# Output projection of the mixing stage: fp32 matmuls replaced by three fp16 products of high and low halves

## The chip, the cores and the metric

The kernel runs on one core of one Trainium2 chip, as one program. The metric is the device time of one execution in microseconds (us). Engine names: PE is TensorE's matmuls, PEld its weight loads, DVE is VectorE, ACT is ScalarE, POOL is GpSimd, SP is SyncE, which here only issues DMAs.

## The reference, cut to what matters

The kernel computes one layer of a hybrid encoder for 4096 prompt frames and 128 frames of eight running streams: a mixing layer, then a mixture of experts, then a norm. What is computed around the change:

```
mixed = concatenate([out_a, o], axis=-1)      # (tokens, 1024): 512 from the LRU group, 512 from the delta-rule heads
x = x + mixed @ w_out                         # w_out: 1024 x 1024, float32
x = x + hier_moe(rmsnorm(x, ln2_g), ...)      # the router reads the normed x
```

`o` is the output of a recurrence over tokens (`gdn_sequence`): each block of tokens needs a triangular inverse and the state that the block before left.

## The kernel before

`build` runs phases one after the other: `project_phase` (input projection, groups of 512 tokens), `mix_phase` (this change), routing, experts, `combine_phase`.

`project_phase` already computes its own projection as three fp16 products: PE lines L292 multiply high by high, low by high and high by low halves of 128x512 tiles. ACT makes the high halves of the weights, DVE the low halves (L467), from a staged fp32 copy.

`mix_phase` handles 33 tiles of 128 tokens (the last one holds the streams). A tile passes three steps, in three consecutive turns: X prepares it (Gram matrices, and a triangular inverse by doubling: levels 1, 2, 4 to 64), Y applies the state and projects, R norms, routes and writes the tile's rows. In one turn the kernel interleaves X of tile t+2, Y of tile t+1 and R of tile t. The order is written out by hand in the list `MIX`: each entry `step.name.engine` is issued in that order on its engine, for each turn. Tiles 0 and 1 and the last ones are written out; those between run in a loop whose body holds two turns (`program`). Each step waits on counters of the steps that it needs (`at(name, t, back)`), so an engine that is ahead waits.

Names that the prediction uses:

- The doubling. `W2`, `W4` to `W64` (PE, L844): product of a masked matrix `Bs` and `Tm`. `I2` to `I64` (DVE, L1166): copies the result out into `WI`, adding the identity. `T2` to `T32` (PE, L854): product of `Zm` and `WI`. `T2c` and so on (ACT, L995, for T1c L991): copies it out into `Tm`. `Z2` to `Z32` (PE, L860): transposes of `Tm`. `Z2c` and so on (ACT, L1003): copies them out into `Zm`. So one level is W, I, T, Tc, Z, Zc, then the next T.
- `outA0` to `outA3` (PE, L923): projection of the LRU half of the features, `ft[p]`, two of the four 128-row chunks and one half of 512 columns each. `outB0` to `outB7` (PE, L935): the heads' half, one head and one column half each, from `mx`. Both accumulate into the banks `YD`, `YE`. In PE's order these stand between the steps of the doubling: one outB between Z and T, one between T and W.
- `oT` (PE, L930) transposes the normed head outputs, `mx` (DVE, L1228) multiplies them by the gate. `o` (DVE, L1221), `so` (ACT, L1025, sums of squares), `ro` (POOL), `on` (DVE, L1225) are the norm before that.
- `x2` (DVE, L1235, L1236) adds the residual, `st` (ACT) stores it and sums squares, `r2` (POOL) and `xn` (DVE, L1241) norm it, `hT0`, `hT1` (PE) and `hc0`, `hc1` (DVE, L1245) turn it for the router `lg` (PE, L947). `h2` (POOL, L1087) is the product that is stored for the experts.
- `S` (DVE, L1214) updates the state, `G` (DVE, L1147) builds the decayed Gram matrix, `Z1` (DVE, L1161 and L1163) starts the doubling, `B2` to `B64` (POOL, L1065) mask `G` for each level. `ATm` (POOL, L1059) masks the attention matrix. `T1` (PE, L833) and `T1c` start the doubling of the tile; `r0`, `r1` (DVE) pick the experts.
- SP issues, in this order: `ft[0]`, router, norm row, token numbers, `xr[0]`, `w_out` (4 MB), the streams' states `S_s` (2 MB, needed by the last tile alone), then in its loop `ft` and `xr` of tile 1 and those that follow (L752 to L758). `ft` of tile t+2 waits until `outA1` and `mx` of tile t are done.

Of the kernel before, what the change touches and what calls it, by code (L numbers as in the profile page):

```python
# [16 lines left out]
FP16 = mybir.dt.float16  # L17
# [559 lines left out]
Y.N.pe Y.vd.dve Y.vh.act  # L577
X.kt.pe X.ktc.act X.vt.pe X.sc.dve
R.hT0.pe R.hT1.pe R.hc0.dve R.hc1.dve
Y.dS.pe Y.S.dve Y.AV.pe  # L580
# [5 lines left out]
X.W2.pe X.I2.dve Y.outA0.pe  # L586
X.T2.pe X.T2c.act Y.outA1.pe Y.oT.pe X.B8.pool
X.W4.pe X.Z2.pe X.Z2c.act Y.mx.dve X.I4.dve Y.outB0.pe X.B16.pool
X.T4.pe X.T4c.act Y.outB1.pe X.B32.pool
X.W8.pe X.Z4.pe X.Z4c.act X.I8.dve R.r3.dve Y.outB2.pe  # L590
# [12 lines left out]
def mix_phase(nc, T, gb, const, cols, eid, rank, wts, base):  # L603
    NT = tiles()
    H = HEADS
    with ExitStack() as ctx:
        def sb(name, shape, dt=FP32):
            return ctx.enter_context(nc.sbuf_tensor(name, shape, dt))

        def sem(name):  # L610
            return ctx.enter_context(nc.semaphore(name))

        w_out = sb("w_out", [P, KD, D])
        router = sb("router", [P, KD, P])
# [73 lines left out]
        flat = lambda b: b[:, :, :].rearrange("p h n -> p (h n)")  # L688

        done = {(st, e): Steps(sem(f"mix_{st}_{e}"), [n for a, n, b in MIX if a == st and b == e], lead=2)  # L690
                for st in "XYR" for e in ENGINES if any(a == st and b == e for a, n, b in MIX)}
        owner = {n: done[st, e] for st, n, e in MIX}
        weights_in = sem("mix_weights_in")
        w_out_in = sem("w_out_in")
        S_s_in = sem("S_s_in")
# [14 lines left out]
        def at(name, t, back=0):  # L710
            return owner[name].at(name, t, back)
# [12 lines left out]

        def program(engine, begin, x_step, y_step):
# [24 lines left out]
        @block.sync  # L750
        def _(sp):
            def load(t, p):  # L752

                sp.wait_ge(*at("outA1", t, 2))
                sp.wait_ge(*at("mx", t, 2))
                sp.dma_start(ft[p][:, :, :], T["mixin"][:, :, bass.ts(t, P)]).then_inc(ft_in[p], 16)
                sp.wait_ge(*at("x2", t, 2))
                sp.dma_start(xr[p][:, :], T["x"][bass.ts(t, P), :]).then_inc(xr_in[p], 16)  # L758

            sp.dma_start(ft[0][:, :, :], T["mixin"][:, :, 0:P]).then_inc(ft_in[0], 16)  # L760
            sp.dma_start(router[:, :, :], T["router"]).then_inc(weights_in, 16)
            sp.dma_start(ln2_row[:, :], T["ln2_row"].to_broadcast([P, D])).then_inc(weights_in, 16)
            sp.dma_start(tok[:, :], T["tokens"]).then_inc(weights_in, 16)
            sp.dma_start(xr[0][:, :], T["x"][0:P, :]).then_inc(xr_in[0], 16)
            sp.dma_start(w_out[:, :, :], T["w_out"]).then_inc(w_out_in, 16)
            sp.dma_start(S_s[:, :, :, :], T["S_s"]).then_inc(S_s_in, 16)
            with sp.Fori(0, (NT - 1) // 2) as pair:
                load(pair * 2 + 1, 1)
                load(pair * 2 + 2, 0)
            sp.wait_ge(S_ready, 1)  # L770
            sp.dma_start(T["out_S_p"], S[:, :, :]).then_inc(S_out, 16)
            sp.wait_ge(S_ready, 2)
            sp.dma_start(T["out_S_s"], S_s[:, :, :, :]).then_inc(S_out, 16)
            sp.wait_ge(S_out, 32)
# [6 lines left out]
        def _(pe):  # L781
# [87 lines left out]
            def y_step(n, t, p, stream, did):  # L869
# [46 lines left out]
                elif n[:-1] == "outA":  # L916
                    half, c0 = divmod(int(n[-1]), 2)
                    if isinstance(t, int) and t == 0:
                        pe.wait_ge(w_out_in, 16)
                    pe.wait_ge(*at("x2", t, 1))  # L920
                    pe.wait_ge(*at("r0" if half == 0 else "hc1", t, 1))
                    for c in (2 * c0, 2 * c0 + 1):
                        ins = nc.tensor.matmul(flat((YD, YE)[half]), ft[p][:, QC + ZC + c, :],  # L923
                                               w_out[:, c, half * 512:half * 512 + 512], start=(c == 0), stop=False)
                    ins.then_inc(*did(n))
# [35 lines left out]
        def _(act):  # L961
# [43 lines left out]
            def y_step(n, t, p, stream, did):  # L1005
# [12 lines left out]
                elif n == "so":  # L1018
# [88 lines left out]
        def _(dve):  # L1107
# [68 lines left out]
            def y_step(n, t, p, stream, did):  # L1176
# [734 lines left out]
```

## Time and profile before

| | |
|---|---|
| Time, median of 3 runs (lowest to highest) | 4360.78 us (4359.83 to 4360.94) |
| The profiled execution, its span | 4364.01 us, 4362.4 us |
| PE, PEld busy (share of the span) | 3795.3 us (87%), 2252.1 us (52%) |
| DVE, ACT, POOL busy | 1899.5 us (44%), 1409.7 us (32%), 843.1 us (19%) |
| Mixing stage | from about 1250 to 2960 us |

A row of the groups by line reads: line, engine, operation, output<-inputs, shapes, xcount | busy us, mean ns of one | idle us of the engine just before them <- what ended it. A row of the timeline reads: start us, duration us, engine, line, operation, names, shapes, xcount [idle before <- releaser]. Rows with a count are merged. An fp32 matmul leaves two records. Matmuls are pipelined: their recorded durations overlap the next one, so a price per matmul is read from start to start.

### The profile page before, as it was taken

The numbers are of one execution on the slowest core, as the hardware profiler recorded it, in microseconds if no ns is written. First come the engines' busy times: TensorE is split into PE (matmuls) and PEld (weight loads), VectorE is DVE, ScalarE is ACT, GpSimd is POOL, SyncE is SP. The second block draws the span as 40 slices with busy tenths as digits, with TensorE's granted clock in tenths as the row PEclk, the third lists the DMA queues.
The fourth block names the chain that finished last, engine by engine and source line by source line (L and its number), as shares of the span: only waits on it lengthen the run. The fifth ranks groups of instructions, "written<-read, shape, count | busy, mean of one in ns | idle before, by whom it ended". The sixth has DMA issues, their size and how long they took to land. (4 is left out here: it accounts for less than half of the span.)

```text
span 4362.4 us, 64251 instructions
## 1 busy us (share of the span) xinstructions
PE 3795.3 (87%) x19068; PEld 2252.1 (52%) x19069; DVE 1899.5 (44%) x4556; ACT 1409.7 (32%) x2749; POOL 843.1 (19%) x853
## 2 busy tenths in 40 slices
PE   7999999999959899889989998965999999999920
PEld 3444444444556666666666676652444444444410
DVE  6555545644535555555555555533111111111147
ACT  6445444544433333333333333300111111111122
POOL 0000000000013333343333333311111111111145
PEclk9999999999979999999999999977999999999965
DMA  4210111010131121112112111103554545553269
GB/s 148 88 66 33 55 48 67 36 53 34 47 121 49 58 65 60 57 59 64 63 56 66 56 63 58 54 20 136 190 186 173 202 178 197 192 186 131 96 276 383
DMA packets 221781, 454.94 MB, mean 104 GB/s; under 512 B 20818, under 2 KB 132818, under 8 KB 213074
## 3 DMA queue, kind: packets, MB, share of 16 engines
q1 hardware_dynamic: 138498, 220.96, 14.9%
q10 hardware_dynamic: 54288, 146.56, 8.5%
q0 software_dynamic: 28864, 86.09, 5.6%
q14 instruction: 100, 0.82, 0.1%
q8 instruction: 31, 0.51, 0.0%
HBM read 303.84 MB, written 149.71 MB: 104 GB/s over the span
## 5 line engine op out<-in xcount | busy, mean ns | idle before, releaser
L1539 PE MATMUL ebank<-w,rowsT 128*128 x1568 | 711.6, 608 | 35.6 <-SPq L1489 32.3
L292 PE MATMUL pP<-h_hi,w_hi 128*128 128x512 f16 (+1 forms) x1728 | 625.0, 366 | 31.5 <-DVE h_lo L474 16.8
L292 PE MATMUL pP<-h_hi,w_lo 128*128 128x512 f16 (+1 forms) x1728 | 624.6, 365 | 0.0
L292 PE MATMUL pP<-h_lo,w_hi 128*128 128x512 f16 (+1 forms) x1728 | 624.5, 365 | 0.0
L1539 PEld LDWEIGHTS ebank<-w,rowsT 128*128 128x128 f32 x1568 | 303.9, 195 | 429.1 <-issue 429.1
L1557 PE MATMUL ebank<-w,guT 128*128 x784 | 353.4, 593 | 2.6 <-ACT guT L1578 2.6
L1606 DVE TENSOR_TENSOR gu<-ebank,sil 128x256 f32<-128x256 f32 x98 | 41.6, 425 | 707.2 <-ACT sil L1574 707.2
L505 DVE SCALAR_TENSOR_TENSOR cv<-win,cols_sb,cv 128x512 f32<-128x512 f32 (+1 forms) x432 | 305.4, 707 | 35.1 <-issue 3.6
L1574 ACT ACTIVATE sil<-ebank 128x256 f32<-128x256 f32 x98 | 37.7, 385 | 829.7 <-PE ebank L1539 829.6
L1166 DVE TENSOR_TENSOR WI<-bank,const 128x512 f32<-128x512 f32 x198 | 136.5, 690 | 376.4 <-PE bank L844 371.9
L292 PEld LDWEIGHTS pP<-h_hi,w_hi 128*128 128x128 f16 x1728 | 172.0, 100 | 220.7 <-issue 30.8
L1065 POOL TENSOR_TENSOR B<-G,const 128x512 f32<-128x512 f32 x198 | 255.8, 1311 | 143.8 <-DVE G L1147 138.8
L844 PEld LDWEIGHTS bank<-Tm,B 128*128 128x128 f32 x1584 | 195.0, 194 | 158.8 <-ACT Tm L995 78.5
L935 PE MATMUL bank<-w_out,mx 128*128 128x512 f32 x528 | 269.5, 594 | 0.8 <-DVE mx L1228 0.8
L292 PEld LDWEIGHTS pP<-h_lo,w_hi 128*128 128x128 f16 x1728 | 172.2, 100 | 187.6 <-issue 13.6
L844 PE MATMUL bank<-Tm,B 128*128 128x128 f32 x1584 | 228.0, 288 | 46.7 <-ACT Tm L991 42.8
L292 PEld LDWEIGHTS pP<-h_hi,w_lo 128*128 128x128 f16 x1728 | 172.1, 100 | 183.0 <-issue 3.0
L923 PE MATMUL bank<-w_out,ft 128*128 128x512 f32 x528 | 247.9, 593 | 0.0
L854 PEld LDWEIGHTS bank<-WI,Zm 128*128 128x128 f32 x1320 | 162.1, 193 | 141.9 <-ACT Zm L1003 71.8
L854 PE MATMUL bank<-WI,Zm 128*128 128x128 f32 x1320 | 192.5, 289 | 47.1 <-DVE WI L1166 33.2
L252 POOL TENSOR_TENSOR ss<-ss,eps 128x4 f32<-128x4 f32 (+1 forms) x9 | 1.8, 200 | 1115.4 <-ACT junk L340 1115.4
L1557 PEld LDWEIGHTS ebank<-w,guT 128*128 128x128 f32 x784 | 140.9, 189 | 143.7 <-issue 143.7
(282 smaller groups left out, 5703.2 us busy)
## 6 DMA issues: line engine op xcount, KB each, us to landing
w<-in_w SPq DMA_DIRECT2D x32, 2048.0 KB, 9.1
y<-yb ACTq DMA_DIRECT2D x98, 512.0 KB, 4.8
ft<-mixin SPq DMA_DIRECT2D x33, 1280.0 KB, 6.3
mixin<-qo ACTq DMA_DIRECT2D x128, 256.0 KB, 2.0
w<-in_w SPq DMA_DIRECT2D x32, 1024.0 KB, 12.3
xt<-in_x SPq DMA_DIRECT2D x33, 512.0 KB, 6.0
xr<-in_x SPq DMA_DIRECT2D x33, 512.0 KB, 4.7
x<-x2b ACTq DMA_DIRECT2D x33, 512.0 KB, 5.0
```

The source lines that it names most:

```text
L292: ins = nc.tensor.matmul(pP[n % NPB][:, 0:N], w[:, k, c0:c0 + P], h[:, k, 0:N], start=(k + i == 0), stop=(k == KD - 1 and i == 2))
L505: ins = nc.vector.scalar_tensor_tensor(dst, window(c, j, stream), cw(j), dst, ALU.mult, ALU.add)
L844: ins = nc.tensor.matmul(XB[:, h, :], Bs[s][:, h, :], Tm[:, h, :], start=True, stop=True)
L854: ins = nc.tensor.matmul(XC[:, h, :], Zm[:, h, :], WI[:, h, :], start=True, stop=True)
L923: ins = nc.tensor.matmul(flat((YD, YE)[half]), ft[p][:, QC + ZC + c, :], w_out[:, c, half * 512:half * 512 + 512], start=(c == 0), stop=False)
L935: nc.tensor.matmul(flat((YD, YE)[half]), mx[:, h, :], w_out[:, LC + h, half * 512:half * 512 + 512], start=False, stop=(h == H - 1)).then_ ...
L1065: nc.gpsimd.tensor_tensor(Bs[s][:, :, :], G[:, :, :], heads(mat(f"level{s}")), ALU.mult).then_inc(*did(n))
L1166: nc.vector.tensor_tensor(WI[:, :, :], XB[:, :, :], heads(mat("ident")), ALU.add).then_inc(*did(n))
L1539: ins = nc.tensor.matmul((M0, M1)[p][:, :], xT[p][:, k, :], w13[:, bass.ds(s, 1), k * 512:(k + 1) * 512].rearrange("p a n -> p (a n)"), st ...
L1557: ins = nc.tensor.matmul((OA, OB)[h][:, :], guT[p][:, k, :], w.rearrange("p a n -> p (a n)"), start=(k == 0), stop=(k == FE // P - 1))
L1574: nc.scalar.activation(sil[p][:, :], (M0, M1)[p][:, 0:FE], ACT.Silu).then_inc(*did(n))
L1606: nc.vector.tensor_tensor(gu[p][:, :], (M0, M1)[p][:, FE:2 * FE], sil[p][:, :], ALU.mult).then_inc(*did(n))
```

## The change

`w_out` is kept as two fp16 arrays of the same total size, `w_out_hi` (512 times the matrix, rounded) and `w_out_lo` (the rest). Its fp32 form is loaded in two halves into the space of `kz` and `S_s`, which the last tile uses; it is split after the first turn (X of tile 0): eight ACT copies and eight DVE subtractions of 128x1024, each engine in its own order. SP waits for the end of the split before it loads `S_s`, and its `ft` loads come behind that.

For each tile, ACT rounds the LRU features (times 4) to `f_hi` (`fh`) and DVE subtracts for `f_lo` (`fl`); ACT rounds `mx` (`mh`) and DVE subtracts (`ml`). Each fp32 matmul of outA and outB becomes three fp16 matmuls. `x2` becomes a multiplication and an addition. `ft` no longer waits for `outA1`. In PE's order `outA1` moves behind `Z2`, and `outB0` behind `T4`, next to `outB1`.

```diff
-X.kt.pe X.ktc.act X.vt.pe X.sc.dve
-R.hT0.pe R.hT1.pe R.hc0.dve R.hc1.dve
+X.kt.pe X.ktc.act X.vt.pe X.sc.dve Y.fh.act
+R.hT0.pe R.hT1.pe R.hc0.dve R.hc1.dve Y.fl.dve
@@
-X.T2.pe X.T2c.act Y.outA1.pe Y.oT.pe X.B8.pool
-X.W4.pe X.Z2.pe X.Z2c.act Y.mx.dve X.I4.dve Y.outB0.pe X.B16.pool
-X.T4.pe X.T4c.act Y.outB1.pe X.B32.pool
+X.T2.pe X.T2c.act Y.oT.pe X.B8.pool
+X.W4.pe X.Z2.pe X.Z2c.act Y.mx.dve Y.mh.act X.I4.dve Y.outA1.pe Y.ml.dve X.B16.pool
+X.T4.pe X.T4c.act Y.outB0.pe Y.outB1.pe X.B32.pool
@@ program
             run((0, 0, False), None, None)
+            if after_first:
+                after_first()
@@ SP
-                sp.wait_ge(*at("outA1", t, 2))
                 sp.wait_ge(*at("mx", t, 2))
@@
-            sp.dma_start(w_out[:, :, :], T["w_out"]).then_inc(w_out_in, 16)
+            for n, half in enumerate(w_out_raw):
+                sp.dma_start(half, T["w_out"][:, n * 4:n * 4 + 4, :]).then_inc(w_out_in[n], 16)
+            sp.wait_ge(w_out_ready, KD)
             sp.dma_start(S_s[:, :, :, :], T["S_s"]).then_inc(S_s_in, 16)
@@ PE
-                        pe.wait_ge(w_out_in, 16)
-                    pe.wait_ge(*at("x2", t, 1))
+                        pe.wait_ge(w_out_ready, KD)
+                    pe.wait_ge(*at("fl", t))
                     pe.wait_ge(*at("r0" if half == 0 else "hc1", t, 1))
                     for c in (2 * c0, 2 * c0 + 1):
-                        ins = nc.tensor.matmul(flat((YD, YE)[half]), ft[p][:, QC + ZC + c, :],
-                                               w_out[:, c, half * 512:half * 512 + 512], start=(c == 0), stop=False)
+                        for i, (w, f) in enumerate(((w_out_hi, f_hi), (w_out_lo, f_hi), (w_out_hi, f_lo))):
+                            ins = nc.tensor.matmul(flat((YD, YE)[half]), f[:, c, :],
+                                                   w[:, c, half * 512:half * 512 + 512], start=(c + i == 0), stop=False)
@@
-                    pe.wait_ge(*at("mx", t))
+                    pe.wait_ge(*at("ml", t))
@@ ACT
+                elif n == "fh":
+                    act.wait_ge(ft_in[p], ft_turn(t, p))
+                    act.wait_ge(*at("outA1", t, 1))
+                    nc.scalar.activation(f_hi[:, :, :], ft[p][:, QC + ZC:FC, :], ACT.Copy, scale=M_SCALE).then_inc(*did(n))
+                elif n == "mh":
+                    act.wait_ge(*at("outB7", t, 1))
+                    act.wait_ge(*at("mx", t))
+                    nc.scalar.activation(mx_hi[:, :, :], mx[:, :, :], ACT.Copy).then_inc(*did(n))
@@
+            def split_out():
+                for k in range(KD):
+                    act.wait_ge(w_out_in[k // 4], 16)
+                    nc.scalar.activation(w_out_hi[:, k, :], w_out_raw[k // 4][:, k % 4, :], ACT.Copy, scale=W_SCALE
+                                         ).then_inc(w_out_hi_ready, 1)
@@ DVE
+                elif n == "ml":
+                    dve.wait_ge(*at("mh", t))
+                    nc.vector.tensor_tensor(mx_lo[:, :, :], mx[:, :, :], mx_hi[:, :, :], ALU.subtract).then_inc(*did(n))
+                elif n == "fl":
+                    dve.wait_ge(*at("fh", t))
+                    nc.vector.scalar_tensor_tensor(f_lo[:, :, :], ft[p][:, QC + ZC:FC, :], M_SCALE, f_hi[:, :, :],
+                                                   ALU.mult, ALU.subtract).then_inc(*did(n))
@@
-                    nc.vector.tensor_tensor(x2b[:, 0:512], flat(YD), xr[p][:, 0:512], ALU.add)
-                    nc.vector.tensor_tensor(x2b[:, 512:], flat(YE), xr[p][:, 512:], ALU.add).then_inc(*did(n))
+                    nc.vector.scalar_tensor_tensor(x2b[:, 0:512], flat(YD), OUT, xr[p][:, 0:512], ALU.mult, ALU.add)
+                    nc.vector.scalar_tensor_tensor(x2b[:, 512:], flat(YE), OUT, xr[p][:, 512:], ALU.mult, ALU.add
+                                                   ).then_inc(*did(n))
@@
+            def split_out():
+                for k in range(KD):
+                    dve.wait_ge(w_out_hi_ready, k + 1)
+                    nc.vector.scalar_tensor_tensor(w_out_lo[:, k, :], w_out_raw[k // 4][:, k % 4, :], W_SCALE,
+                                                   w_out_hi[:, k, :], ALU.mult, ALU.subtract).then_inc(w_out_ready, 1)
```

## Rows read from the trace of the kernel before

**Rows 1.** The page's costliest groups: the heads' half of the projection.

```profile
L935 PE MATMUL bank<-w_out,mx 128*128 128x512 f32 x528 | 269.5, 594 | 0.8 <-DVE mx L1228 0.8
```

**Rows 2.** Timeline of PE, tile 0's doubling, no projection between the steps.

```profile
1301.41 0.60 PE L860 MATMUL bank<-const,Tm 128*128 128x128 f32 x4
1302.79 1.13 PE L854 MATMUL bank<-WI,Zm 128*128 128x128 f32 x8 [0.78 <-ACT Zm L1003]
1304.70 1.13 PE L844 MATMUL bank<-Tm,B 128*128 128x128 f32 x8 [0.78 <-ACT Tm L995]
```

**Rows 3.** Timeline of PE, tile 1's doubling, an outB between the steps.

```profile
1337.80 0.60 PE L860 MATMUL bank<-const,Tm 128*128 128x128 f32 x4
...
1339.18 1.13 PE L854 MATMUL bank<-WI,Zm 128*128 128x128 f32 x8
1340.14 1.02 PE L935 MATMUL bank<-w_out,mx 128*128 128x512 f32 x2
1341.09 1.13 PE L844 MATMUL bank<-Tm,B 128*128 128x128 f32 x8
```

**Rows 4.** Timeline of PE, a turn in the loop: T2, oT, W4, Z2, T4, W8.

```profile
2003.63 1.16 PE L854 MATMUL bank<-WI,Zm 128*128 128x128 f32 x8 [0.51 <-DVE WI L1166]
...
2006.35 0.60 PE L930 MATMUL bank<-const,onb 128*128 128x128 f32 x4
2006.79 1.06 PE L844 MATMUL bank<-Tm,B 128*128 128x128 f32 x8
2007.68 0.60 PE L860 MATMUL bank<-const,Tm 128*128 128x128 f32 x4
...
2008.98 1.15 PE L854 MATMUL bank<-WI,Zm 128*128 128x128 f32 x8
...
2010.82 1.15 PE L844 MATMUL bank<-Tm,B 128*128 128x128 f32 x8
```

**Rows 5.** Timeline of ACT, the same turn: T4c.

```profile
2010.16 0.60 ACT L995 ACTIVATE Tm<-bank 128x512 f32<-128x512 f32 x1 [1.25 <-PE bank L854]
```

**Rows 6.** Timeline of PE, the same turn: T1 and W2 with their waits.

```profile
1996.55 0.66 PE L833 MATMUL bank<-const,Zm 128*128 128x128 f32 x4 [0.96 <-DVE Zm L1163]
...
2000.24 1.16 PE L844 MATMUL bank<-Tm,B 128*128 128x128 f32 x8 [1.31 <-ACT Tm L991]
```

**Rows 7.** Timeline of DVE: x2's second half, Z1's first part, mx, and on one turn later.

```profile
1982.20 0.68 DVE L1236 TENSOR_TENSOR x2b<-bank,xr 128x512 f32<-128x512 f32 x1
...
1994.00 1.73 DVE L1161 TENSOR_TENSOR B<-G,const 128x512 f32<-128x512 f32 x1 [0.16 <-issue]
...
2006.99 0.75 DVE L1228 SCALAR_TENSOR_TENSOR mx<-bank,cols_sb,ft 128x512 f32<-128x512 f32 x1 [3.41 <-PE bank L930]
...
2050.82 1.76 DVE L1225 TENSOR_TENSOR onb<-ob,ro 128x512 f32<-128x512 f32 x1
```

**Rows 8.** Timeline of POOL, the same turn: B2, then B8 to B64.

```profile
1993.92 1.27 POOL L1065 TENSOR_TENSOR B<-G,const 128x512 f32<-128x512 f32 x1 [4.17 <-DVE G L1147]
...
2004.06 4.95 POOL L1065 TENSOR_TENSOR B<-G,const 128x512 f32<-128x512 f32 x4
```

**Rows 9.** Timeline of PE, input projection: two fp16 matmuls in a run.

```profile
600.25 0.38 PE L292 MATMUL pP<-h_lo,w_hi 128*128 128x512 f16 x1
600.47 0.38 PE L292 MATMUL pP<-h_hi,w_lo 128*128 128x512 f16 x1
```

**Rows 10.** Groups by line and form: DVE's low half of 128x1024 weights.

```profile
L467 DVE SCALAR_TENSOR_TENSOR w_lo<-stage,w_hi 128x1024 f16<-128x1024 f32 x24 | 29.2, 1221 | 11.0 <-ACT w_hi L348 11.0
```

**Rows 11.** Timeline of ACT: sq of tile 1, directly behind Z64c of tile 0.

```profile
1308.76 1.05 ACT L966 ACTIVATE sqb<-ft 128x1024 f32<-128x1024 f32 x1
```

**Rows 12.** The page's DMA issues: KB each, median us from issue to landing.

```profile
ft<-mixin SPq DMA_DIRECT2D x33, 1280.0 KB, 6.3
```

**Rows 13.** Windows: PE, PEld, DVE, ACT, POOL busy, granted clock, DMA share, GB/s.

```profile
1256.00:1280.00 24.00, 13.19 (x70) 12.09 (x71) 6.77 (x22) 5.24 (x10) 9.87 (x7) 0.64 1.03 407
```

**Rows 14.** Timeline of PE, first work of the mixing stage.

```profile
1261.78 3.75 PE L793 MATMUL bank<-const,sqb 128*128 128x128 f32 x16 [17.54 <-DVE gs L1115]
```

More of the change, by code:

```diff
@@ L44 @@
 PROJ = 1.0 / (W_SCALE * H_SCALE)
+M_SCALE = 4.0
+OUT = 1.0 / (W_SCALE * M_SCALE)
 W13, W2 = KD * 2 * FE, (FE // P) * D
@@ L611, in sem @@
             return ctx.enter_context(nc.semaphore(name))
-        w_out = sb("w_out", [P, KD, D])
+        w_out_hi = sb("w_out_hi", [P, KD, D], FP16)
+        w_out_lo = sb("w_out_lo", [P, KD, D], FP16)
+        f_hi = sb("f_hi", [P, LC, P], FP16)
+        f_lo = sb("f_lo", [P, LC, P], FP16)
+        mx_hi = sb("mx_hi", [P, H, P], FP16)
+        mx_lo = sb("mx_lo", [P, H, P], FP16)
+        ng4 = sb("ng4", [P, 1])
         router = sb("router", [P, KD, P])
@@ L688, in mix_phase @@
         flat = lambda b: b[:, :, :].rearrange("p h n -> p (h n)")
+        w_out_raw = [kz[:, :, :, :].rearrange("p h s n -> p (h s n)").rearrange("p (k n) -> p k n", k=4),
+                     S_s[:, :, :, :].rearrange("p s h n -> p (s h n)").rearrange("p (k n) -> p k n", k=4)]
         done = {(st, e): Steps(sem(f"mix_{st}_{e}"), [n for a, n, b in MIX if a == st and b == e], lead=2)
@@ L693, in mix_phase @@
         weights_in = sem("mix_weights_in")
-        w_out_in = sem("w_out_in")
+        w_out_in = [sem(f"w_out_in{n}") for n in range(2)]
+        w_out_hi_ready = sem("w_out_hi_ready")
+        w_out_ready = sem("w_out_ready")
         S_s_in = sem("S_s_in")
@@ L723, in col, with program @@
             return cols[:, COLS[name][0] + n:COLS[name][0] + n + w]
-        def program(engine, begin, x_step, y_step):
+        def program(engine, begin, x_step, y_step, after_first=None):
             for (st, e), d in done.items():
@@ L932, in y_step @@
                 elif n[:-1] == "outB":
-                    pe.wait_ge(*at("mx", t))
+                    pe.wait_ge(*at("ml", t))
                     half, h = divmod(int(n[-1]), H)
-                    nc.tensor.matmul(flat((YD, YE)[half]), mx[:, h, :], w_out[:, LC + h, half * 512:half * 512 + 512],
-                                     start=False, stop=(h == H - 1)).then_inc(*did(n))
+                    for i, (w, f) in enumerate(((w_out_hi, mx_hi), (w_out_lo, mx_hi), (w_out_hi, mx_lo))):
+                        ins = nc.tensor.matmul(flat((YD, YE)[half]), f[:, h, :],
+                                               w[:, LC + h, half * 512:half * 512 + 512],
+                                               start=False, stop=(h == H - 1 and i == 2))
+                    ins.then_inc(*did(n))
                 elif n in ("hT0", "hT1"):
@@ L1042, in y_step @@
                     nc.scalar.activation(exd[:, NGR:], dif[:, NGR:], ACT.Exp).then_inc(*did(n))
-            program("act", act, x_step, y_step)
+            def split_out():
[3 more added lines that the diff above has]
+                                         ).then_inc(w_out_hi_ready, 1)
+            program("act", act, x_step, y_step, split_out)
         @block.gpsimd
@@ L1227, in y_step @@
                     dve.wait_ge(*at("oT", t))
-                    nc.vector.scalar_tensor_tensor(mx[:, :, :], YC[:, :, :], col("ng"), ft[p][:, QC:QC + ZC, :],
+                    dve.wait_ge(*at("mh", t, 1))
+                    nc.vector.scalar_tensor_tensor(mx[:, :, :], YC[:, :, :], ng4[:, 0:1], ft[p][:, QC:QC + ZC, :],
                                                    ALU.mult, ALU.mult).then_inc(*did(n))
+                elif n == "ml":
[5 more added lines that the diff above has]
+                                                   ALU.mult, ALU.subtract).then_inc(*did(n))
                 elif n == "x2":
@@ L1320, in _ @@
             dve.sem_inc(x2_out, 16)
+            nc.vector.tensor_scalar(ng4[:, :], col("ng"), M_SCALE, None, ALU.mult)
             dve.drain()
-            program("dve", dve, x_step, y_step)
+            def split_out():
[3 more added lines that the diff above has]
+                                                   w_out_hi[:, k, :], ALU.mult, ALU.subtract).then_inc(w_out_ready, 1)
+            program("dve", dve, x_step, y_step, split_out)
             dve.drain()
```

## The prediction

> **What bounds the kernel now.** The page comes first. PE is busy 87% of the span, and the projection's second half is one of its larger groups, with only 0.8 us of idle time before it in the whole run [rows 1]. Read alone, this says that PE is full and that every matmul saved is time saved. The timeline says otherwise. Tile 0 goes through the doubling with no projection in between: from Z to T it takes 1302.79 - 1301.41 = 1.38 us, from T to W 1304.70 - 1302.79 = 1.91 us, and PE waits 0.78 us in each for ACT's copy [rows 2]. Tile 1 goes through the same steps with an outB in each place: 1339.18 - 1337.80 = 1.38 us and 1341.09 - 1339.18 = 1.91 us [rows 3]. An outB costs nothing there; it lies in the wait for the copy. In the loop the steps are 2008.98 - 2007.68 = 1.30 us and 2010.82 - 2008.98 = 1.84 us [rows 4], and T4c, which W8 needs, runs from 2010.16 to 2010.76 [rows 5], so W8 starts 0.06 us behind it. PE has a filler that just fits, no queue.
>
> Third, the waits before T1, W2 and T2: 0.96 us for DVE's `Zm`, 1.31 us for ACT's `Tm`, 0.51 us for DVE's `WI` [rows 4, 6]. outA2, outA3 and outA0 are the work directly ahead of these three. So what sets the turn is a chain through DVE and ACT (x2, st, r2, xn, the scales, hc, S, G, Z1, o, so, T1c, then the levels of the doubling), and PE is only a link of it.
>
> **The matmuls that become shorter.** From T2 to oT lie eight records of T2 and four of outA1: 2.72 us [rows 4]. The eight of W4 take 2007.68 - 2006.79 = 0.89 us; those of a T about 0.98. That leaves 1.74 us for four records, 0.43 each, two to a product: 0.87 us. A fp16 matmul of this width follows the one before it in 600.47 - 600.25 = 0.22 us [rows 9], three take 0.65. PE is given back 0.22 us a product, 16 products and 3.5 us a tile, about 115 us in 33 tiles. Of that, outA2, outA3 and outA0 only lengthen waits that are there already, and the outB of the levels from 8 up lie in the waits for Tc and Zc: gain 0. The bounds are 0.02 us a step for these (what separates filler and copy), so at most 0.2 us a tile, and the full 3.5 if I read the chain wrongly (a rival below).
>
> **The part that is rearranged, T2 to W8.** Now 2010.82 - 2003.63 = 7.19 us [rows 4]. After: W4 no longer stands behind outA1, only behind oT (0.44 us), so its own chain sets it, 1.84 us behind T2 instead of 3.16. Z2 follows 0.89 later, its transposes take 0.44, outA1 1.30: T4 at T2 + 4.47 (its chain would allow 1.84 + 0.89 + 1.30 = 4.03). T4 takes 0.98, outB0 and outB1 1.30: W8 at T2 + 6.75 (its chain: 6.31). That is a gain of 0.44 us, if outB0 doesn't wait. It now waits for `ml`: Z2c ends at T2 + 3.97, `mh` takes 0.60 like the other copies of 512 columns, `ml` 0.68 like x2's [rows 7], so T2 + 5.3, just ahead of 5.45. `mh` has T4c behind it in ACT's order, which can't start before T2 + 5.65; `ml` has I8 behind it, which is later. `mx` gets a wait for `mh` of the tile before, long past.
>
> But POOL is at B8 to B64 until 2009.01, which is T2 + 5.38 [rows 8]. Z1's product reads two arrays in SBUF like `ml`; it began 0.08 us behind B2 and took 1.73 us, until 0.54 us after B2 was done, though `mx`, with one input in SBUF, took its 0.75 us in the middle of POOL's work [rows 7, 8]. So `ml` ends near T2 + 5.92, outB0 starts at 5.97, W8 at 7.27: a loss of 0.08. In the other turn of the loop's two, `on` is held up this way already (1.76 us instead of 0.68), T2 comes 1.1 us later, and POOL is done before `ml`: there the gain of 0.44 stands. Mean: -0.18 us a tile.
>
> The Trainium skill, page "SBUF — State Buffer", section "Who interferes with whom", has this as a rule: a DVE instruction with two SBUF inputs and a GpSimd instruction that reads SBUF exclude each other, and the one that issues first holds the ports for its whole length. The trace agrees, with the 1.73 us of Z1's product. Without the rule the two turns would both gain 0.44 and the sum below would be 8 us lower.
>
> **Additions to the chain.** `fl` stands in DVE's order between hc1 and S, and S, G, Z1, o, r0, r1, on and I2 are queued behind it; DVE goes through them with no wait that it could use, and T1 waits for Z1. Its price is a scalar_tensor_tensor of 512 columns: 0.75 us recorded [rows 7], and some 0.07 less from start to start, as recorded ends overlap; I take 0.68 and keep 0.60 to 0.75. POOL is idle at that point (it waits 4.17 us for G [rows 8]), so nothing holds it. `fh` (ACT, 0.6 us) stands in a wait of ACT for the scales and costs nothing; without that cover it would be 0.6 us more. `x2` changes from 0.68 to 0.75 us, twice, 0.14 us, and st, r2, xn and the scales follow it. Sum +0.82 us on T1, and T1c, W2 and T2 move with it. Its earliest start isn't bound by outB7, so a shorter outB7 gives nothing back.
>
> A tile: +0.82 - 0.18 = +0.64; 32 turns: +20.5 us. Bounds: `on` is held in one turn of two, and that is a matter of some 10 ns between DVE and POOL. In every turn it would be 32 x 0.38 + 17 = +29, in none 32 x 0.90 - 17 = +12.
>
> **The start.** The split runs behind Z64c of tile 0, where ACT now goes straight on to sq of tile 1, at 1308.76 [rows 11]. Both halves of `w_out` have landed by then. ACT makes eight halves of 1.0 us, DVE follows with eight of 1.22 us [rows 10]: 1309.9 + 9.8 = 1319.7. The costlier part is SP. It waits for this before it issues `S_s`, and `ft` and `xr` of tile 1 are queued behind that: `ft` is issued near 1320.5, behind 2 MB of `S_s`. At the 407 GB/s of the busiest window [rows 13], `S_s` takes 5.2 us, and `ft` 6.3 from issue to landing [rows 12]: 1332, so sq is 23 us late. From below 18 (ft's 6.3 alone), from above 32 (half of that rate for both). PE idles about 22 us in it. After 17.5 idle us the first 16 records took 3.75 us [rows 14], at 1.2 GHz, half the speed; half of them and part of the next groups are lost again: +2.6, from 0 up to 10, if it falls back as in the window with a granted clock of 0.64 [rows 13]. Sum +26, bounds 18 to 42. PE's new wait in outA of tile 0 for the split costs nothing behind this.
>
> **The end.** In the last tile nothing else runs, so both projections are on the path: -1.7 us each. `mh` and `ml` come between mx and outB: +1.4. Together -2.
>
> **Sum.** +20.5 + 26 - 2 = +44.5 us. The profiled execution had 4364.0 us (its span 4362.4), 3 us over the median; on the median of 4360.8 the forecast is 4405 us. Chance 0.67. Its own range is 4385 (start 18, turns +8) to 4430 (start 32, turns +29, some clock).
>
> **Rivals.** PE is the bound after all: then DVE's additions are hidden and the whole saving counts, 4361 - 115 + 26 = 4272 us. For it speaks PE's 87%; against it rows 2 and 3, where the same steps take the same time with and without an outB. It decides if the waits before T1, W2 and T2 are gone. Chance 0.04.
>
> The clock: the waits before T1 and W2 grow from 0.96 and 1.31 to 2.1 and 1.75 us. Now PE has the full clock all through the loop; if it falls to 1.2 GHz at this place in most turns, T2's 0.98 us double while they are on the chain: +1 us a tile, 4437 us. Chance 0.14.
>
> `fl` is hidden (DVE had slack before S): 32 x (0.14 - 0.18) + 24 = 4384 us. Against it: DVE works from hc to Z1 almost without idle time. Chance 0.08.
>
> The start is covered and so is `fl` (S_s doesn't hold `ft`, and ACT's split lies in a wait): 4361 + 5, no change. Chance 0.05. The last 0.02 are for what I haven't seen. That the matmuls don't become three fp16 products is excluded by the code.
>
> **Range and chances.** Main case and hidden `fl` reach from 4384 to 4430; with part of the clock case the range is 4384 to 4433 us. A difference within 0.2% (9 us) can't be told from no change: faster 0.05, same 0.05, slower 0.90.
>
> **What would show each step.** Right: L935 and L923 become 792 records each with starts 0.22 us apart; PE's busy share falls while the turn grows from about 48.3 to 48.9 us; T to W stays 1.84 and Z to T 1.30 us; the waits before T1 and W2 are near 2.1 and 1.75 us; `ml` takes about 1.3 us in every second turn; sq of tile 1 starts near 1332. Wrong: a turn near 45 us (PE was the bound), a turn of 48.3 with DVE idle before S (`fl` hidden), a granted clock below 1 inside the loop, or sq of tile 1 before 1320.

## The result, and the profile after

| | before | after |
|---|---|---|
| Time, median of 4 runs (lowest to highest) | 4360.66 us (4359.83 to 4360.94) | 4417.22 us (4414.18 to 4423.02) |
| Ratio to before, 95% interval | | 1.0132 (1.0114 to 1.0149) |
| Profiled execution, its span | 4364.01 us, 4362.4 us | 4423.02 us, 4421.4 us |

The change makes the kernel 56.6 us slower; 44.5 were forecast (4405 us), with a range of 4384 to 4433 us. The page of the kernel after:

```profile
span 4421.4 us, 65569 instructions
PE 3767.3 (85%) x19596; PEld 2273.0 (51%) x19597; DVE 1969.3 (45%) x4631; ACT 1451.6 (33%) x2823; POOL 838.3 (19%) x853
L953 PE MATMUL bank<-w_out_hi,mx_hi 128*128 128x512 f16 x264 | 100.1, 379 | 1.8 <-DVE mx_lo L1267 1.8
```

PE has less to do and the span is 59.0 us longer, DVE has 70 us more. L953 is one of the three fp16 products that stand in the place of [rows 1]: 0.8 us of waiting became 1.8, nothing beside the 59. So the time is not at the projection itself. Where it is, the starts of `T1c` tell, one per tile (timeline of ACT; tiles 0, 1 and 32; first the kernel before, then the kernel after):

```profile
1275.36 0.60 ACT L991 ACTIVATE Tm<-bank 128x512 f32<-128x512 f32 x1 [4.14 <-PE bank L833]
...
1325.08 0.58 ACT L991 ACTIVATE Tm<-bank 128x512 f32<-128x512 f32 x1
...
2819.70 0.60 ACT L991 ACTIVATE Tm<-bank 128x512 f32<-128x512 f32 x1
```

```profile
1276.91 0.60 ACT L1011 ACTIVATE Tm<-bank 128x512 f32<-128x512 f32 x1 [4.14 <-PE bank L849]
...
1356.18 0.58 ACT L1011 ACTIVATE Tm<-bank 128x512 f32<-128x512 f32 x1
...
2882.44 0.60 ACT L1011 ACTIVATE Tm<-bank 128x512 f32<-128x512 f32 x1
```

The stage begins 1.6 us later. Tile 0's turn goes from 49.72 to 79.27 us (+29.6), the next 31 turns from 1494.62 to 1526.26 (+31.6), and the rest gives back 3.7. Below, "turn 0" and "31 turns" are these two differences.

**Turn 0.** Timelines of ACT, SP and PE after:

```profile
1314.33 0.60 ACT L1019 ACTIVATE Zf<-bank 128x512 f32<-128x512 f32 x1 [1.37 <-PE bank L882]
...
1318.61 3.89 ACT L1075 ACTIVATE w_out_hi<-S_s 128x1024 f16<-128x1024 f32 x4
1337.20 1.06 ACT L986 ACTIVATE sqb<-ft 128x1024 f32<-128x1024 f32 x1 [14.71 <-DMA ft<-mixin]
```

```profile
1325.10 0.33 SPq L782 DMA_DIRECT2D S_s<-in_S_s  x1
1325.81 0.60 SPq L770 DMA_DIRECT2D ft<-mixin  x1
```

```profile
1338.40 3.75 PE L809 MATMUL bank<-const,sqb 128*128 128x128 f32 x16 [22.38 <-ACT sqb L986]
```

ACT is done with its halves at 1322.5 and then waits 14.71 us for `ft`, issued behind `S_s` at 1325.81. PE is idle for 22.38 us, and its first 16 records take 3.75 us, at 1.2 GHz, as in [rows 14].

**The turns.** Here is one in which the clock held; timeline of PE from T1 to W8, the answer to [rows 4, 6]:

```profile
2190.26 0.66 PE L849 MATMUL bank<-const,Zm 128*128 128x128 f32 x4 [1.98 <-DVE Zm L1197]
...
2193.95 0.49 PE L860 MATMUL bank<-Tm,B 128*128 128x128 f32 x2 [1.74 <-ACT Tm L1011]
...
2198.44 1.16 PE L870 MATMUL bank<-WI,Zm 128*128 128x128 f32 x8 [2.04 <-DVE WI L1200]
...
2200.28 1.16 PE L860 MATMUL bank<-Tm,B 128*128 128x128 f32 x8 [0.25 <-ACT Tm L1015]
...
2203.01 1.05 PE L870 MATMUL bank<-WI,Zm 128*128 128x128 f32 x8
...
2205.20 1.05 PE L860 MATMUL bank<-Tm,B 128*128 128x128 f32 x8
```

W4 is at T2 + 1.84, T4 at + 4.57, W8 at + 6.76 us. But T2 now waits 2.04 us for `WI`. In the kernel before it waited 0.51 us in the turn of [rows 4], and 1.62 us in a turn in which `on` was held (2053.23). DVE in the same turn, with `fl` behind hc, then `dif` (a step of `r1`, 128x4) and `on`:

```profile
2183.59 1.29 DVE L1288 TENSOR_TENSOR hT<-bank,cols_sb 128x512 f32<-128x512 f32 x2
2184.80 0.68 DVE L1270 SCALAR_TENSOR_TENSOR f_lo<-ft,f_hi 128x512 f16<-128x512 f32 x1
2185.39 1.11 DVE L1248 SCALAR_TENSOR_TENSOR S<-S,ex,bank 128x128 f32<-128x128 f32 x4
...
2194.73 1.31 DVE L1318 TENSOR_SCALAR dif<-gpad,m 128x4 f32<-128x4 f32 x1
...
2196.03 1.76 DVE L1259 TENSOR_TENSOR onb<-ob,ro 128x512 f32<-128x512 f32 x1
```

The first `dif` takes 1.31 us and `on` 1.76 us, both held by POOL, and T2 comes 5.14 us behind `T1c`; where POOL holds only one operation of DVE there, it comes 4.04 us behind. "`on` is held" below means such a turn of 5.14. In the kernel before there were 14 of them among the loop's 30 turns, as [rows 7] shows for one; here there are 29. What one costs, two like turns of the kernel before tell: tile 10's took 48.10 us with `on` held, tile 6's 46.99 us without.

The third part is the clock. Windows over the middle of the loop, before and then after (PE, PEld, DVE, ACT, POOL busy, granted clock, DMA share, GB/s):

```profile
1420.00:2700.00 1280.00, 1154.66 (x7363) 866.76 (x7362) 709.91 (x2175) 427.44 (x1083) 460.58 (x427) 1.00 0.19 60
```

```profile
1420.00:2700.00 1280.00, 1106.08 (x7623) 865.45 (x7622) 745.97 (x2173) 446.16 (x1117) 447.36 (x416) 0.97 0.19 59
```

The granted clock was 1.00 throughout and now is not: 19 stretches, 85.3 us together, are at 1.2 GHz. Twelve of them begin ahead of W4 and lengthen the turn; the other seven lie at the end of a turn and don't lengthen it or the next (from W8 to the next `T1c` it is 36.27 us with one and 36.28 without). PE in one of the twelve, from T2 to T4:

```profile
2345.59 1.16 PE L870 MATMUL bank<-WI,Zm 128*128 128x128 f32 x8 [2.04 <-DVE WI L1200]
2346.58 0.90 PE L947 MATMUL bank<-const,onb 128*128 128x128 f32 x4
2347.43 2.08 PE L860 MATMUL bank<-Tm,B 128*128 128x128 f32 x8
...
2351.46 0.72 PE L870 MATMUL bank<-WI,Zm 128*128 128x128 f32 x5
```

W4 takes 2.08 us instead of 1.16, and T4 comes at T2 + 5.87 instead of + 4.57. 12 of 31 turns look like this; W8 comes 1.23 to 1.41 us later in each, 15.7 us together.

### The profile page after: what moved, and what is told of

Its sections match the earlier page's. It is cut to its first block and busy times, and to the rows that moved or that the text cites. A ratio compares the mean times of both kernels' runs of the same rounds, so it can differ in the third digit from the quotient of the medians.

```text
span 4421.4 us, 65569 instructions
## 1 busy us (share of the span) xinstructions
PE 3767.3 (85%) x19596; PEld 2273.0 (51%) x19597; DVE 1969.3 (45%) x4631; ACT 1451.6 (33%) x2823; POOL 838.3 (19%) x853
## 5 line engine op out<-in xcount | busy, mean ns | idle before, releaser
L860 PE MATMUL bank<-Tm,B 128*128 128x128 f32 x1584 | 249.3, 305 | 59.4 <-ACT Tm L1011 45.6
L860 PEld LDWEIGHTS bank<-Tm,B 128*128 128x128 f32 x1584 | 215.4, 209 | 141.3 <-ACT Tm L1011 65.6
L294 PEld LDWEIGHTS pP<-h_hi,w_hi 128*128 128x128 f16 x1728 | 172.3, 100 | 221.3 <-issue 31.6
L1023 ACT ACTIVATE Zm<-bank 128x512 f32<-128x512 f32 x165 | 98.5, 597 | 312.7 <-PE bank L876 312.7
L1662 DVE COPY yb<-ebank 128x512 f32<-128x512 f32 x98 | 67.8, 692 | 272.8 <-PE ebank L1608 272.8
```

What stands on the lines that cost most here:

```text
L294: ins = nc.tensor.matmul(pP[n % NPB][:, 0:N], w[:, k, c0:c0 + P], h[:, k, 0:N], start=(k + i == 0), stop=(k == KD - 1 and i == 2))
L860: ins = nc.tensor.matmul(XB[:, h, :], Bs[s][:, h, :], Tm[:, h, :], start=True, stop=True)
L1023: nc.scalar.activation(Zm[:, :, :], XA[:, :, :], ACT.Copy).then_inc(*did(n))
L1662: nc.vector.tensor_copy(yb[p][:, 512:], OB[:, :]).then_inc(*did(n))
```

## The experiments

Each ran beside the kernel before on the same chip; that median stands in brackets. Ratios are to it, with a 95% interval. The parts (turn 0, the 31 turns) are of one profiled execution of each kernel. That of the changed kernel was its slowest (4423.02 us, median 4417.22), that of e1 its fastest (4391.01, median 4400.05), so a difference between such parts carries some us of doubt.

**e1_split_hidden: the split of the features, off the chain.** The kernel after; `fh` and `fl` one turn earlier, behind `T8c` and `I16`.

```diff
-X.kt.pe X.ktc.act X.vt.pe X.sc.dve Y.fh.act
-R.hT0.pe R.hT1.pe R.hc0.dve R.hc1.dve Y.fl.dve
+X.kt.pe X.ktc.act X.vt.pe X.sc.dve
+R.hT0.pe R.hT1.pe R.hc0.dve R.hc1.dve
...
-X.T8.pe X.T8c.act Y.outB3.pe X.B64.pool
-X.W16.pe X.Z8.pe X.Z8c.act X.I16.dve R.rk.pe
+X.T8.pe X.T8c.act Y.outB3.pe X.B64.pool X.fh.act
+X.W16.pe X.Z8.pe X.Z8c.act X.I16.dve X.fl.dve R.rk.pe
```

> The features of a tile are split one turn earlier, in the middle of the doubling: fh behind T8c on ACT, fl behind I16 on DVE, where both engines wait. Theory (fl is a link of the chain, 0.6 us a turn): hc to S back from 1.81 to 1.21 us, 32 x 0.6 = 19 us less than the changed kernel, about 4398 us, and up to 16 us less still if the shorter wait before T1 keeps the clock up. Rival (DVE has slack there, the growth is elsewhere): 4417 us as before.

Measured: 4400.05 us (4362.24), 1.0095 (1.0078 to 1.0112). The 31 turns took 1505.46 us, 20.8 less. Timeline of DVE:

```profile
2267.19 1.29 DVE L1288 TENSOR_TENSOR hT<-bank,cols_sb 128x512 f32<-128x512 f32 x2
2268.40 1.11 DVE L1252 SCALAR_TENSOR_TENSOR S<-S,ex,bank 128x128 f32<-128x128 f32 x4
```

From hc to S it is 1.21 us, with `fl` it was 1.80. `fl` in its place costs 0.6 us a turn, about 19 of the 20.8; `on` was still held in 27 turns, two fewer, which is the other 2. The wait before T1 fell from 1.98 to 1.38 us, but the clock was still low at T4 in 11 turns: that wait alone doesn't decide it, and the further 16 us that were thought possible didn't come.

**e2_start, e11_ft_first: the start.** e11 is the kernel after with one change in SP's order, shown here. e2 has the same and also splits `w_out` chunk by chunk between the copies of tile 0's doubling.

```diff
+            load(1, 1)
             sp.wait_ge(w_out_ready, KD)
             sp.dma_start(S_s[:, :, :, :], T["S_s"]).then_inc(S_s_in, 16)
-            with sp.Fori(0, (NT - 1) // 2) as pair:
+            load(2, 0)
+            with sp.Fori(1, (NT - 1) // 2) as pair:
```

> w_out is split chunk by chunk inside the doubling of tile 0 (ACT behind each copy out of T2 to Z16, DVE behind I4 to I32), and ft and xr of tile 1 are issued ahead of SP's wait for the split and of S_s. The turns stay as they are. Theory (the start costs about 30 us: 29.6 in the turn of tile 0): sq of tile 1 back near 1310, 4417 - 29 = 4388 us. Rival (the split itself is long, or the DMAs of tile 1 are late for another reason): less than 10 us come back.

> The changed kernel with SP's order alone changed: ft and xr of tile 1 are issued ahead of the wait for the split and of S_s. The split of w_out stays one block behind tile 0's X. This parts the 30 us of the start into its two costs. Theory (SP's queue is the costlier part): sq of tile 1 starts as soon as ACT's split ends, near 1319 instead of 1335, and the turn of tile 0 falls from 79.3 to 60 or 64 us: 4417 - 16 = 4401 us. Rival (the split itself, with DVE behind ACT, is the cost): less than 5 us come back.

Measured: e2 4389.89 us (4362.24), 1.0068 (1.0051 to 1.0085), turn 0 54.29 us; e11 4400.13 us (4357.53), 1.0096 (1.0078 to 1.0115), turn 0 61.85 us. ACT in e11:

```profile
1314.22 3.88 ACT L1077 ACTIVATE w_out_hi<-S_s 128x1024 f16<-128x1024 f32 x4
1318.00 1.04 ACT L988 ACTIVATE sqb<-ft 128x1024 f32<-128x1024 f32 x1
```

The 14.71 us of waiting are gone. Turn 0 is made up as follows. Tile 0's doubling, from T1c to Z64c, took 32.91 us in the kernel before, 37.42 in the one after and 34.77 in e11: PE stayed at 1.2 GHz longer. With this taken off, e11's turn 0 is 17.4 - 2.7 = 14.7 us shorter, just the wait behind `S_s`. Of turn 0's 29.6 us that leaves 29.6 - 14.7 - 4.5 = 10.4 for ACT's split (7.6) and the first block at 1.2 GHz (2.7). e2 hides the split too; 4.2 of the 4.6 us that it keeps are in the doubling. But the doubling also took 32.91 us in e3, which is the kernel after up to tile 1, and in e1 and e9. So it isn't shown that the 4.5 us belong to the change; they may be those of the one profiled execution. What decides how long the clock stays low there is open.

**e3_fill: more work for PE.** The kernel after, with a fourth fp16 product, low by low, in the three outA ahead of the waits.

```diff
-                        for i, (w, f) in enumerate(((w_out_hi, f_hi), (w_out_lo, f_hi), (w_out_hi, f_lo))):
+                        parts = ((w_out_hi, f_hi), (w_out_lo, f_hi), (w_out_hi, f_lo), (w_out_lo, f_lo))
+                        for i, (w, f) in enumerate(parts[:3 if n == "outA1" else 4]):
```

> outA2, outA3 and outA0 get a fourth product (low by low), 1.3 us more PE work a tile, in the waits before T1, W2 and T2 alone. Theory (the clock falls in 12 of 31 turns since PE idles more there, and each fall costs some 1.3 us between W4 and T4): the granted clock stays full in the loop and the time is 4417 - 16 = 4401 us with more work. Rival (the falls have another cause, such as the wait between oT and W4): the falls stay, 4417 us. Rival (PE is the bound): 4417 + 40.

Measured: 4404.08 us (4362.24), 1.0095 (1.0078 to 1.0111). Its window over the loop:

```profile
1420.00:2700.00 1280.00, 1119.25 (x7907) 870.37 (x7905) 753.63 (x2201) 453.40 (x1131) 450.95 (x421) 1.00 0.19 60
```

PE has six matmuls more to do a turn, 1.3 us, and the 31 turns are 17.4 us shorter (1508.91). The waits before W2 and T2 fell from 1.74 and 2.04 to 1.31 and 1.61 us, and the granted clock was 1.00. `on` was held in 29 turns, as in the kernel after. This puts a size on the clock: 17.4 us, beside the 15.7 us read from the twelve turns.

**e4_half_outB: is PE the bound?** The kernel before, outB only 256 of its 512 columns wide; the other half of the heads' product is left out.

```diff
-                    nc.tensor.matmul(flat((YD, YE)[half]), mx[:, h, :], w_out[:, LC + h, half * 512:half * 512 + 512],
+                    nc.tensor.matmul(flat((YD, YE)[half])[:, 0:256], mx[:, h, :], w_out[:, LC + h, half * 512:half * 512 + 256],
```

> The kernel before, with each outB product computed for 256 of its 512 columns: half of that product is left out, 8 x 0.43 us of PE work a tile, 113 us in all. Theory (an outB lies in the wait for a copy): the steps T to W and Z to T stay 1.84 and 1.30 us and the time stays 4361 us, or rises a little where the clock falls. Rival (PE is the bound): 4361 - 113 = 4248 us.

Measured: 4358.76 us (4362.24), 0.9994 (0.9984 to 1.0003). Timeline of PE:

```profile
2006.92 1.16 PE L854 MATMUL bank<-WI,Zm 128*128 128x128 f32 x8 [0.25 <-ACT Zm L1003]
...
2008.77 1.16 PE L844 MATMUL bank<-Tm,B 128*128 128x128 f32 x8 [0.25 <-ACT Tm L995]
```

T to W is still 1.85 us. Each shorter outB turned into a wait of 0.25 for ACT's copy. outB loses 0.43 us a product, twice what the change saves (0.22), and the kernel takes the same time. For outA, e3 shows the same from the other side: more work there cost no time.

**e9_before_order: the order alone.** The kernel before, in fp32, with PE's new order.

```diff
-X.T2.pe X.T2c.act Y.outA1.pe Y.oT.pe X.B8.pool
-X.W4.pe X.Z2.pe X.Z2c.act Y.mx.dve X.I4.dve Y.outB0.pe X.B16.pool
-X.T4.pe X.T4c.act Y.outB1.pe X.B32.pool
+X.T2.pe X.T2c.act Y.oT.pe X.B8.pool
+X.W4.pe X.Z2.pe X.Z2c.act Y.mx.dve X.I4.dve Y.outA1.pe X.B16.pool
+X.T4.pe X.T4c.act Y.outB0.pe Y.outB1.pe X.B32.pool
```

> The kernel before with nothing but PE's new order: outA1 behind Z2, outB0 behind T4 with outB1, all products fp32. Theory (the order alone moves PE work behind steps whose own chains are 1.84 and 1.30 us; only the shorter fp16 products make it a gain): W4 at T2 + 1.84, T4 at + 4.9, W8 at + 7.6 instead of 7.19, 0.4 us a turn or 13 us more, 4374 us, if on is held in every second turn as before; 17 us more if the order is what makes it held in every turn. Rival (the order is the gain, the fp16 products add nothing): W8 at T2 + 6.76, 4347 us.

Measured: 4367.17 us (4359.73), 1.0021 (1.0011 to 1.0031). W8 at 2018.88 behind T2 at 2011.28:

```profile
2011.28 1.16 PE L854 MATMUL bank<-WI,Zm 128*128 128x128 f32 x8 [0.51 <-DVE WI L1166]
...
2018.88 1.05 PE L844 MATMUL bank<-Tm,B 128*128 128x128 f32 x8
```

That is 7.60 us, 0.41 longer than before. In the new order T4 stands behind outA1 and W8 behind outB0 and outB1, in fp32 1.74 us each time; it is the fp16 form (1.30) that turns this into 6.76. The measured 7.4 us are less than the 13 expected. `on` was held in 15 turns, so the order isn't what changed the pattern.

**e10_both_hidden: e1 and e2 together.**

> The changed kernel with both of its costs taken off the path, as the two runs that did each alone: w_out split inside tile 0's doubling with ft of tile 1 ahead of S_s, and the features split one turn earlier; POOL's order is not touched. Theory (the two are independent, 27 and 17 us): 4417 - 44 = 4373 us, of which some 17 us is on held in every turn. Rival (with the start gone or fl gone something else takes over): 4385 us or more.

Measured: 4379.08 us (4359.73), 1.0048 (1.0031 to 1.0065), 6 us over the 4373 expected: turn 0 53.83, the 31 turns 1506.81, the clock low at T4 in 12, `on` held in 29. With `fl` and the start both out of the way, the kernel is still 19 us slower than before. What remains is the held `on`, the clock and the 4.2 us of tile 0's doubling.

**e5_on: POOL's order around `on`.** The kernel after; B4 ahead of `ro`, and `ATm` and the later masks out of the way (`y` is false where there is no Y step).

```diff
-R.lg.pe Y.so.act Y.ro.pool R.r0.dve R.sh.act
-Y.outA2.pe X.B4.pool
+R.lg.pe Y.so.act X.B4.pool Y.ro.pool R.r0.dve R.sh.act
+Y.outA2.pe
...
-Y.outA3.pe X.ATm.pool
+Y.outA3.pe
...
-X.T8.pe X.T8c.act Y.outB3.pe X.B64.pool
+X.T8.pe X.T8c.act Y.outB3.pe X.B64.pool X.ATm.pool
...
+                    if s == 8 and y:
+                        pool.wait_ge(*at("on", t, 1))
+                    if s == 32 and y:
+                        pool.wait_ge(*at("ml", t, 1))
```

> The changed kernel with POOL's masks moved: B4 ahead of ro, B8 and B16 wait for on, B32 and B64 and then ATm wait for ml. Theory (POOL's B4, issued 0.03 us before or behind DVE's dif, holds dif and on in every turn, where before it did so in every second one; that is the largest part of the turns' growth): on takes 0.68 us, T2 comes 4.04 us behind T1c in all turns instead of 5.14, W8 stays at T2 + 6.76: 1.1 us a turn, 4417 - 34 = 4383 us; more falls of the clock would not follow, since PE idles less. Rival (DVE's own instructions are long there, POOL only coincides): 4417 us.

Measured: 4371.76 us (4362.72), 1.0016 (1.0005 to 1.0027). Timeline of DVE:

```profile
2070.99 0.21 DVE L1323 TENSOR_SCALAR dif<-gpad,m 128x4 f32<-128x4 f32 x1
...
2071.20 0.69 DVE L1264 TENSOR_TENSOR onb<-ob,ro 128x512 f32<-128x512 f32 x1
```

`on` is 0.69 us in all turns, but the first `dif` also fell, from 1.31 to 0.21. T2 comes 2.99 us behind T1c instead of 5.14 in 19 of the 30 turns. The gain is smaller than 2.15 a turn, since B4 now holds up Z1's second product: S to T1 goes from 4.87 to 5.77 us. 2.15 - 0.90 = 1.25 us a turn; the 31 turns took 1488.40, 37.9 less.

The clock, expected not to fall more often, did. PE now waits 2.88 us before T1, and the clock falls there (timeline of PE, and the window over the loop):

```profile
2017.57 1.11 PE L849 MATMUL bank<-const,Zm 128*128 128x128 f32 x4 [2.88 <-DVE Zm L1202]
```

```profile
1420.00:2700.00 1280.00, 1137.54 (x7829) 883.82 (x7827) 754.69 (x2241) 459.10 (x1152) 461.20 (x428) 0.96 0.20 60
```

22 stretches, 105.8 us together, are at 1.2 GHz, and in the other 11 turns T2 comes 4.0 to 5.1 us behind T1c. That costs some 16 us, about as much as the twelve turns of the kernel after (15.7), so the two cancel in the 37.9.

**e6_before_pool, e7_pool: all of POOL's holds.** The same order on the kernel before (with `mx` for `ml`) and on the kernel after, and two waits more, for `Z1` and for the scales:

```diff
+                    pool.wait_ge(*at("Z1", t))
...
+                    if not isinstance(t, int) or t + 2 < NT:
+                        pool.wait_ge(*at("sc", t, -2))
                     pool.wait_ge(*at("xn", t))
```

> The kernel before, with POOL kept out of DVE's way: besides the order of the run before (mx in the place of ml), B2 waits for Z1, and h2 waits for the scales of the tile that X prepares. Theory (DVE instructions with two SBUF inputs wait for the POOL instruction that is running): the scales' first product falls from 2.31 to 0.16 us, Z1's from 1.73 to 0.69, on is never held: about 3.7 us a turn until PE binds, 4361 - 118 = 4243 us. Rival (the chain is bound by PE or ACT beside DVE): less than 40 us.

> The changed kernel with the same three edits on POOL. Theory: turn 48.8 - 2.15 - 1.04 - 1.1 = 44.5 us, about 4417 - 137 = 4280 us. The fp16 products now have some worth, as PE is nearer to being the bound: the difference to the run before of this call is that of the turns and the start alone, 4280 - 4243 = +37 us, or less where PE binds there. Rival (PE binds in both): the changed kernel is the faster one by up to 3.5 us a tile less 30 us, 4243 - 82 us.

Measured: e6 4219.49 us (4362.72), 0.9665 (0.9648 to 0.9682), the 31 turns 1360.24; e7 4264.44 us (4362.72), 0.9786 (0.9768 to 0.9805), the 31 turns 1384.67. e6 gained more than expected: the two holds at `dif` and `on`, of which only one was counted, both went. e7 came out 16 us under the 4280 expected. In e6 PE binds; it has no idle time before T2:

```profile
1981.87 1.05 PE L854 MATMUL bank<-WI,Zm 128*128 128x128 f32 x8
```

In e7 `fl` costs more than before, since `h2` now runs beside it (timeline of DVE):

```profile
1997.46 1.29 DVE L1296 TENSOR_TENSOR hT<-bank,cols_sb 128x512 f32<-128x512 f32 x2
1998.67 1.92 DVE L1278 SCALAR_TENSOR_TENSOR f_lo<-ft,f_hi 128x512 f16<-128x512 f32 x1
```

**e8_all: e7 with e2 and e1.**

> The run before of this call, and w_out split inside tile 0's doubling with ft of tile 1 ahead of S_s, and the features split one turn earlier. Theory: 25 us less at the start, 0.6 us less a turn: 4280 - 44 = 4236 us, about as fast as the kernel before with the same POOL edits, or faster where PE binds that one. Rival (with DVE relieved, PE's idle time keeps the clock down or another wait takes over): 4265 us or more.

Measured: 4191.21 us (4362.72), 0.9608 (0.9592 to 0.9624), lowest to highest 4188.63 to 4194.11. Turn 0 took 44.25 us, the 31 turns 1330.84. That is 45 us under the 4236 expected. It beats both kernels, and e6 by 28 us (29.4 of them in the 31 turns): the fp16 form pays once POOL no longer holds DVE and the split lies off the path.

## Why the prediction was right

The time is in the range and the likeliest case came in, but only in part by its own mechanism. The saved matmul time was hidden and the start grew, as worked out. The growth of the turns was added up from `fl` and `x2`, and it came from `on` and from the clock. That the sum stayed where it was forecast is in part luck: without the further holds of `on` and the falls of the clock (16.5 and 15.7 us, below) it would have been about 4417.2 - 16.5 - 15.7 = 4385 us, at the range's lower end. Step by step:

- **PE isn't the bound, outB's saving is worth nothing.** Right. e4 halves outB and comes to 0.9994 (0.9984 to 1.0003).
- **T2 to W8.** Right: 6.76 us where 6.75 was worked out, W4 at + 1.84 as given, T4 at + 4.57 for + 4.47. Where `on` was not held, `ml` was held by POOL as forecast: 1.30 us, and W8 at T2 + 7.29 for 7.27. But this was forecast for every second turn and came in one of the loop's, tile 3 (timelines of DVE and PE; POOL's four masks run from 1456.96 to 1461.91):

```profile
1461.16 1.30 DVE L1267 TENSOR_TENSOR mx_lo<-mx,mx_hi 128x512 f16<-128x512 f32 x1 [0.89 <-ACT mx_hi L1055]
```

```profile
1456.53 1.16 PE L870 MATMUL bank<-WI,Zm 128*128 128x128 f32 x8 [0.91 <-DVE WI L1200]
...
1463.82 0.94 PE L860 MATMUL bank<-Tm,B 128*128 128x128 f32 x7
```

- **`fl` and `x2`.** `fl` 0.60 from start to start where 0.68 was taken. `x2` was put 0.14 too high: a scalar_tensor_tensor with a constant as its scalar takes 0.68 us like the addition it replaced. The 0.75 of `mx` in [rows 7] belongs to a form with a column of scalars. The page of the kernel after has both of the new ones:

```profile
L1270 DVE SCALAR_TENSOR_TENSOR f_lo<-ft,f_hi 128x512 f16<-128x512 f32 x33 | 22.5, 682 | 1.4 <-ACT f_hi L1051 1.4
L1278 DVE SCALAR_TENSOR_TENSOR x2b<-bank,xr 128x512 f32<-128x512 f32 x33 | 22.5, 681 | 0.0
```

- **The turn.** Wrong in its two parts, and 11 us low in its sum. Measured for 31 turns +31.6 us, forecast for 32 +20.5. The edits themselves cost nearly nothing: a turn with `on` held and the clock full took 48.10 us before and 48.17 after (+0.60 for `fl`, -0.43 for T2 to W8, some -0.1 elsewhere), where +0.38 was forecast for such a turn. With `on` held in half the turns the forecast would thus have been too high. The 31.6 are two other things. `on` was held in 29 turns, not 14: 15 times 1.1 = 16.5 us; the term was taken at one turn in two, and "in every turn" stood only as the bound of +29. And the clock fell in 12 turns: 15.7 us by the later W8, 17.4 by e3. The two make 32.2 us and leave nothing for the edits.
- **The clock rival** was given 0.14 for "most turns". It came in 12 of 31, at 1.3 us each for 1, so a rival's mechanism gave about a quarter of the whole loss; "a granted clock below 1 inside the loop" was one of the prediction's own signs of being wrong. The waits it was argued from were right (1.98 and 1.74 us for 2.1 and 1.75); what it left out is that T2's wait grows too, to 2.04 us.
- **The start.** +26 forecast, 29.6 measured: sq 22.4 us later behind the doubling (23 forecast), 2.7 for the clock in the first block (2.6), and the 4.5 in tile 0's doubling that were not in the sum and aren't shown to be of the change. The mechanism is as forecast: e11, which moves `ft` ahead of `S_s` and nothing else, takes the 14.7 us of waiting away.
- **The end.** -2 forecast. From tile 32's T1c to the end of its last product on POOL, `h2`, it went from 119.08 to 116.21 us, -2.9. All that follows T1c gives -3.7, but this is 1538.9 us here and 1543.3 in e3, so that figure can't size a term of 2.

Why `on` was held more often is only half settled. Here are DVE and POOL of the kernel before in a turn where it was not held:

```profile
2001.02 0.21 DVE L1275 TENSOR_SCALAR dif<-gpad,m 128x4 f32<-128x4 f32 x1
2001.14 1.24 DVE L1276 TENSOR_TENSOR dif<-m8e 128x1 f32<-128x1 f32 x1
2002.30 0.68 DVE L1225 TENSOR_TENSOR onb<-ob,ro 128x512 f32<-128x512 f32 x1
```

```profile
2001.05 1.31 POOL L1065 TENSOR_TENSOR B<-G,const 128x512 f32<-128x512 f32 x1
2002.32 1.78 POOL L1059 TENSOR_TENSOR AT<-AT,const 128x512 f32<-128x512 f32 x1
```

B4 holds up a `dif` either way. If the first gets through, the second is held, and then `on` comes ahead of `ATm`. If the first is held, `ATm` comes ahead of `on`, for 1.1 us more. In the loop's turns, tile 3's apart, the first `dif` starts 20 to 30 ns ahead of B4 in the records, in turns of both kinds and in both kernels. So what tips it is too small for these records. It isn't the order of PE alone (e9, 15 turns) nor the length of outB (e4, 15); whatever else the change shifts, it was held in 27 to 29 turns in e1, e2, e3 and e10. That the hold is what costs the time is shown, by e5. The Trainium skill, page "SBUF — State Buffer", section "Who interferes with whom", says that issue order and not shape decides who blocks. As to the shape the trace agrees: an operation of 128x1 is held for 1.24 us where it takes 0.15. As to the order it can't tell, since `dif` starts first in the records whether it is held or not.

## What to carry to other kernels

Before a matmul is made cheaper, measure whether it is work or filler: compare the same steps with and without it. When PE waits longer, count what its clock may do as a cost of its own, and read the granted clock of the loop. A cost that two engines settle between them in every second turn can go to every turn: carry both ends of it in the forecast. Where DVE and GpSimd share a chain, look for DVE operations that take several times their usual duration: here their removal was worth 143 us (e6), and the change itself gained only behind it.

## What the runs showed of the hardware

- Small operations on DVE are held too: `dif` with one input in SBUF and a column of scalars (128x4) took 1.31 us beside a POOL product, 0.21 without. The scales' product of 128x4 took 2.30 us in e1 and 0.16 in e8.

```profile
2264.17 2.30 DVE L1167 TENSOR_TENSOR sc<-sse,rr 128x4 f32<-128x4 f32 x1 [0.27 <-POOL rr L1090]
```

```profile
1996.04 0.16 DVE L1178 TENSOR_TENSOR sc<-sse,rr 128x4 f32<-128x4 f32 x1 [0.27 <-POOL rr L1093]
```

- PE's clock fell behind waits of 2 us. In the kernel after it fell in 12 turns, with waits of 1.98, 1.74 and 2.04 us before T1, W2 and T2, and in e1 in 11 turns with 1.38, 1.74 and 2.04. It stayed full through the loop in e3 (1.55, 1.31 and 1.61), and in the kernel before, e4 and e9 (0.96, 1.32 and at most 1.62). In e5 it fell with 2.88 us before T1.
